# Eighty-six extra matmuls, whose results nobody reads, ahead of the first stick-breaking scores

## What is computed

```python
hn = _rmsnorm(h, norm_mix[layer])
q, k, v = jnp.split(hn @ w_qkv_a[layer], 3, axis=-1)   # 16 heads of 64
z = einsum('bhqd,bhkd->bhqk', qb, kh) * scale          # scores
log_stay = where(strict, log_sigmoid(-z), 0.0)
log_after = cumsum(log_stay, reverse=True) - log_stay
w = where(strict, exp(log_sigmoid(z) + log_after), 0.0)
o = einsum('bhqk,bhkd->bhqd', w, vh)
h = h + o @ w_o_a[layer]
h = h + (silu(f @ w_gate) * (f @ w_up)) @ w_down       # f = rmsnorm(h)
```

## Time and profile before

| what | value |
|---|---|
| time, median of 2 runs | 2456.45 us (2456.35 to 2456.56) |
| span of the profiled execution | 2456.5 us |
| PE busy | 2418.6 us (98% of the span), 11642 matmuls |
| PEld busy | 1974.2 us (80%) |
| DVE busy | 1394.3 us (57%) |
| ACT busy | 908.5 us (37%) |
| granted TensorE clock, mean | 0.996 of full speed |

### The profile page before, as it was taken

How to read it: one execution, slowest core, us unless ns; L and a number is a source line. 1 busy time by engine, 2 the same in 40 slices (tenths; PEclk the granted TensorE clock), 3 DMA queues, 4 the chain that set the end, 5 groups by cost and what they waited for, 6 DMA issues and landing times.

```text
span 2456.5 us, 31236 instructions
## 1 busy us (share of the span) xinstructions
PE 2418.6 (98%) x11642; PEld 1974.2 (80%) x11642; DVE 1394.3 (57%) x2270; ACT 908.5 (37%) x1299; POOL 159.8 (7%) x171
## 2 busy tenths in 40 slices
PE   9999999999999999999999999999999999999998
PEld 8777888888777788888788887888888877888886
DVE  4676555433666555542366765766643665766643
ACT  4454322223666432222333332533321564433312
POOL 0000000000000000000020000000030451000031
PEclk9999999999999999999999999999999999999999
DMA  4112222223122233222311112222223312322232
GB/s 173 61 60 78 95 94 94 86 94 103 61 69 69 86 97 100 94 77 94 122 68 68 51 68 95 86 94 94 93 87 106 135 53 78 103 94 94 85 112 94
DMA packets 61078, 218.93 MB, mean 89 GB/s; under 512 B 6805, under 2 KB 7349, under 8 KB 60864
## 3 DMA queue, kind: packets, MB, share of 16 engines
q1 hardware_dynamic: 58464, 208.28, 25.5%
q0 software_dynamic: 2064, 8.97, 1.0%
q10 hardware_dynamic: 464, 0.48, 0.1%
HBM read 215.59 MB, written 2.12 MB: 89 GB/s over the span
## 4 chain that ended last, share of the span: by engine, by line
PE 88%; DVE 6%; ACT 4%; issue 1%; DMA 0%; DVEq 0%; SPq 0%; ACTq 0%
PE ps L261 25%; PE ps L263 25%; PE ps L262 25%; PE ps L2001 2%; DVE stick_left L1386 1%; PE ps L1063 1%; DVE stick_p L1392 1%; PE ps L300 1%; PE ps L301 1%; ACT window_p L1667 1%; PE ps L305 1%; PE ps L1190 1%; PE ps L1051 1%; PE ps L1210 1%; PE ps L1077 1%
## 5 line engine op out<-in xcount | busy, mean ns | idle before, releaser
L261 PE MATMUL ps<-xh,wh 128*128 128x512 f32 x1832 | 729.3, 398 | 3.9 <-DVE wl L255 2.1
L263 PE MATMUL ps<-xh,wl 128*128 128x512 f32 x1832 | 715.1, 390 | 0.0
L262 PE MATMUL ps<-xl,wh 128*128 128x512 f32 x1832 | 714.2, 390 | 0.0
L247 ACT ACTIVATE wh<-raw 128x1024 fp32r<-128x1024 f32 x331 | 347.8, 1055 | 507.4 <-PE ps L263 470.8
L255 DVE TENSOR_TENSOR wl<-raw,wh 128x1024 fp32r<-128x1024 f32 x331 | 408.1, 1234 | 200.2 <-ACT wh L247 198.4
L261 PEld LDWEIGHTS ps<-xh,wh 128*128 128x128 f32 x1832 | 344.8, 188 | 77.8 <-issue 6.5
L263 PEld LDWEIGHTS ps<-xh,wl 128*128 128x128 f32 x1832 | 344.5, 188 | 73.1
L262 PEld LDWEIGHTS ps<-xl,wh 128*128 128x128 f32 x1832 | 345.0, 188 | 70.4 <-issue 2.2
L261 PE MATMUL ps<-wh,up_ah 128*128 128x512 f32 x528 | 205.7, 390 | 1.1 <-DVE wl L428 1.1
L262 PE MATMUL ps<-wl,up_ah 128*128 128x512 f32 x528 | 205.4, 389 | 0.0
L263 PE MATMUL ps<-wh,up_al 128*128 128x512 f32 x528 | 205.4, 389 | 0.0
(11 more groups left out here) (300 smaller groups left out, 3307.8 us busy)
## 6 DMA issues: line engine op xcount, KB each, us to landing
raw<-weights SPq DMA_DIRECT2D x387, 512.0 KB, 3.5
cst<-rows_d POOLq DMA_DIRECT2D x9, 512.0 KB, 4.8
hgrn_mask<-levels POOLq DMA_DIRECT2D x1, 2048.0 KB, 7.8
window_bias<-bias_rows POOLq DMA_DIRECT2D x1, 2048.0 KB, 9.4
hT<-x_t SPq DMA_DIRECT2D x7, 256.0 KB, 6.4
out_t<-hT SPq DMA_DIRECT2D x7, 256.0 KB, 2.1
cst<-consts SPq DMA_DIRECT2D x1, 832.0 KB, 8.9
raw<-weights SPq DMA_DIRECT2D x2, 256.0 KB, 4.1
```

The source lines that it names most:

```text
L247: act.activation(wh[slot][:, :], raw[slot][:, :], ACT.Copy).then_inc(hi_done, 1)
L261: pe.matmul(out, w_hi, m_hi, start=first, stop=False, **kw)
L262: pe.matmul(out, w_hi, m_lo, start=False, stop=False, **kw)
L263: return pe.matmul(out, w_lo, m_hi, start=False, stop=last, **kw)
```

## The change

A function `forms(pe)` is added and called once in `stick_pe`, between the wait for the values' copies and the first two key tiles of pair 1. Everything that it issues is on TensorE; nothing is added on another engine and no semaphore is added. All operands are `xh` (stationary) and `xl` (moving), and all results go to banks 2 and 3, which the first scores write over with `start=True`.

```diff
+        def forms(pe):
+
+            whole = xl[:, :, :].rearrange("p j s -> p (j s)")
+            for shift in (0, 16, 64, 256):
+                for j in range(KT):
+                    pe.matmul(ps[:, 2, :], xh[:, j, shift:shift + P], xl[:, j, :], start=True, stop=True)
+            for shift in (16, 64):
+                for j in range(KT - 1):
+                    pe.matmul(ps[:, 2, :], xh[:, j, 0:P], whole[:, j * S + shift:(j + 1) * S + shift],
+                              start=True, stop=True)
+            for j in range(KT):
+                for part in range(2):
+                    rows = slice(part * HD, (part + 1) * HD)
+                    pe.matmul(ps[:, 2 + part, :], xh[rows, j, 0:P], xl[rows, j, :], start=True, stop=True)
+            for j in range(KT):
+                pe.matmul(ps[0:HD, 2, :], xh[:, j, 0:HD], xl[:, j, :], start=True, stop=True)
+            for j in range(KT):
+                pe.matmul(ps[:, 2, :], xh[:, j, 0:P], xl[:, j, 0:2].rearrange("p (a b) -> p a b", a=1).broadcast_to([P, S // 2, 2]),
+                          start=True, stop=True)
+            for j in range(KT):
+                pe.matmul(ps[:, 2, 0:384], xh[:, j, 0:P], xl[:, j, 0:384], start=True, stop=True)
@@
             stick_project(pe, a, sq_slab(0), 1, range(KT))
             pe.wait_ge(a.v_ready, 2 * SB)
+            forms(pe)
             stick_project(pe, a, sk_slab(1), key_bank(1), range(0, 2))
```

## The result

| | before | changed kernel |
|---|---|---|
| time, median of 2 runs, us | 2456.45 | 2475.18 (2474.4 and 2475.97) |
| ratio | | 1.0075, 95% interval 1.0045 to 1.0104 |
| span of the profiled execution, us | 2456.5 | 2472.6 |
| PE busy, us | 2418.6 | 2434.6 |

The change costs 0.7%, within the 2% that count as the same. The forecast was 2474.4 us with a range of 2470.9 to 2481.0. Measured again later in five rounds against the kernel before, the ratio was 1.0071 (1.0057 to 1.0085); the sum in the prediction gives 1.0073.

A forecast was written before the change was run, and what follows sets the result against it. The prediction took TensorE, busy 98% of the span with no hole at the place, as the bound. Pitches of 86 matmuls (14.05 + 1.81 + 1.39) plus 0.60 for mode changes gave 17.85 us on 2456.5: 2474.4 us, range 2470.9 to 2481.

The forecast's parts named there:

- changes of mode: In the new block, three switches (128 rows to 64, to 64 columns, back to full), some 0.2 us each, 0.60 together.
- signs that the prediction gave for being wrong: L1228 starting every 0.2 us, L1232 or a shifted form pitched longer, clock falling, or end shift unlike that at 85 us.
- TensorE bounds the kernel at this place: Between pair 0's queries and pair 1's keys TensorE has no hole; until 205 us only 1.4 us are free.
- The price is the pitch, and 0.2267 us for 512 columns: Each new TensorE matmul costs its start-to-start distance: 0.2267 us for 512 columns, 0.1733 for 384.
- Shifts are free: In the new block, 32 matmuls with shifted stationary and 14 with shifted moving operands cost the plain 0.2267 us each.
- Two halves of the rows run beside each other; 64 columns on one half don't, and their loads are hidden: In the new block, 16 matmuls on 64 rows cost 1.81 us as 8 pairs; eight with 64 columns cost 0.2267 each.
- The repeated pair costs the plain price: In the new block, eight matmuls whose moving operand repeats a pair of elements cost the plain 0.2267 us each.
- half-speed case: The eight repeated-pair matmuls read at half speed, + 1.7 us; among the dearer forms, 2476 to 2481 us, together 0.15.
- Nothing is given back: Behind the block everything starts 17.85 us later and no idle time absorbs it; partly absorbed (under 2473) had 0.02.
- The profiled span is the time: For the kernel before, the profiled span of 2456.5 us was taken as the median of the runs, 2456.45.
- The loads stand in the open: In the block each weight load waits for the matmul ahead: 0.40 us each, 2491 us; 0.04 including the lower clock.
- the clock falls: Granted clock drops to 1.2 GHz with 64-row or 64-column forms, at most doubling 17.85 us: 2492; 0.04 including open loads.

## Why the prediction was right, point by point

The mechanism was right: the new matmuls stand in a stream without a hole, and each costs its pitch. That the sum hits the block within 0.12 us is in part luck. The changes of mode were put 0.25 us too high and the repeated pair 0.09, and the other forms ran over by 0.2 in all. Two of the signs that the prediction gave for being wrong did come: a shifted form has a slightly longer pitch of its own, and the shift at the end (16.14 us) is not that at 85 us (17.74).

*TensorE bounds the kernel at this place.* Right: block and shift of the scores are the same 17.7 us, and the stretch behind has 138.62 us of busy time in 140, 138.60 before.

*The price is the pitch, and 0.2267 us for 512 columns.* Right within 2% for the shifted stationary (7.33 us for 32), and 0.175 for 384 columns against 0.173.

*Shifts are free.* Nearly right. With the stationary operand shifted by 0 or 256 columns the pitch is 0.227, by 16 it is 0.233 and by 64 0.230. The moving one costs 0.231; the group of 14 takes 0.16 us more than forecast, 0.09 of which is the first step into the mode behind it.

*Two halves of the rows run beside each other; 64 columns on one half don't, and their loads are hidden.* Both right, and shown with the halves apart (save for the banks). The size of the changes of mode was too large: three times 0.2 were forecast, and 0.2, 0.15 and 0 were found. The row on which the 64-column changes rested was one with float32 operands, and its 0.10 and 0.12 don't carry over to float32r.

*The repeated pair costs the plain price.* It cost less, 0.215. The argument for it was weak: I took the HGRN levels with runs and gaps of 1 and of 16 elements, 1.00 us both the earlier trace rows, as rows that show no loss. At 512 float32r columns the gaps do cost twice the price. The HGRN rows have 64 columns in 0.11 us, so long a pitch that half speed can hide in it. Had the form been a gap and not a repeat, the term would have been wrong by 1.8 us. The prediction named this weakness and kept the half-speed case in its range.

*Nothing is given back.* Right where it can be told: two blocks cost 17.73 and 17.77 us, and with the same dips a block of 17.3 us moves the end by as much. The prediction had no term for the dips, since it read the 9 in every slice as a full clock. The kernel before had one at 1968 us that alone moved the shift by 2.7 us. Whether the block keeps the dip at 806 us away, 1.4 us, is open.

*The profiled span is the time.* The prediction set 2456.5 equal to the median time of 2456.45. That is a coincidence: with 1.8 us between span and time, that execution took some 2458.3 us, more than its kernel's median. It did no harm, since span and median give the same start for the sum.

*The loads stand in the open* and *the clock falls*, the two dear rivals: the block is dense, at 1.00, with no pitch near 0.40.

## What to carry to other kernels

Where TensorE is 98% busy, a matmul costs its distance from start to start (here columns / 2.4 ns plus 13 ns), not the duration in its row, and it costs it in full; the same matmul in a hole costs nothing, which the starts on both sides of the hole show. For float32r operands as here, let the moving operand run in aligned groups of four elements, and put matmuls on 64 rows in turns on both halves. A difference of spans of 1 to 3 us in this kernel is within what the dips of the clock do in one execution (30 executions of the kernel before spanned 2453.6 to 2457.9), so compare stretches, or executions whose dips stand at the same places.

## What the runs showed of the hardware that was not expected

- A moving operand of float32r that uses only 2 of each aligned 4 elements streams at half speed: 0.45 us for 512 columns instead of 0.227; four of four, in runs of 4, 8 or 16 with gaps as long, 0.231 to 0.241.
- Repeats of 2 to 8 elements stream faster than contiguous data: 0.215 us, nearly 512 columns at 2.4 GHz (0.213).
- The granted clock falls to its lower level behind holes of which the longest lasted 1.7 to 2.2 us (2.18 us at 804, 1.69 at 1224 and 1.75 at 1966) in some executions of a program and not in others; the dip at 1968 us cost 2.7 us.
- Changing between 128 and 64 rows costs 0.2 us, between 128 and 64 columns nothing that the steps show.
